# Two token tiles of the expert picks scattered instead of three, and four through the one-hot gates instead of three

## What is computed

```
s1, s2 = q1 @ key1.T, q2 @ key2.T            # 128 scores each
v1, i1 = top_k(s1, 16);  v2, i2 = top_k(s2, 16)
sc, pos = top_k(all 256 sums v1 + v2, 16)
experts = i1[pos // 16] * 128 + i2[pos % 16]
gate = softmax(sc)
act = gelu(u[experts] . x_t) * gate
out_t = sum over picks of act * v[experts]
```

## Time and profile before

| | us |
|---|---|
| median of three runs | 4469.14 (4467.87 to 4476.68) |
| the profiled execution, its own time | 4451.02 |
| its span, first to last instruction | 4449.4 |
| head stage, first query tile to the end of the bridge | 1964.2 to 2484 |
| gate stage, to the last gate matmul | 2484 to 3017 |
| tail | 3017 to 3361 |
| expert sums and final norm | 3361 to 4449 |

### The profile page before, as it was taken

The page is one execution under the profiler, slowest core; times in us unless marked ns, Lnnn a source line. Parts: engine busy times, 40 slices in busy tenths (PEclk is TensorE's granted clock), DMA queues, the critical chain, the costliest instruction groups (busy, mean ns, idle before and its releaser), DMA issues.

```text
span 4449.4 us, 63937 instructions
## 1 busy us (share of the span) xinstructions
PE 4185.1 (94%) x22555; PEld 3563.2 (80%) x22555; DVE 3044.1 (68%) x6114; ACT 1557.6 (35%) x2721; POOL 1466.3 (33%) x1221
## 2 busy tenths in 40 slices
PE   7999999999899889989999998898798999999998
PEld 4668877777688768779999988888797888888886
DVE  7531037777467744447888688885468998888888
ACT  4222226555477633232223444442121222222222
POOL 0000000000044411002888788888753222222220
PEclk9999999999999989999999999999899999999999
DMA  6646323333456465233445699999898988888885
GB/s 266 243 167 244 141 76 130 117 131 113 156 173 191 141 227 184 95 106 93 93 89 108 171 267 261 262 277 273 235 347 315 303 304 285 288 288 285 287 286 197
DMA packets 479233, 913.43 MB, mean 205 GB/s; under 512 B 188818, under 2 KB 270114, under 8 KB 475412
## 3 DMA queue, kind: packets, MB, share of 16 engines
q1 hardware_dynamic: 321524, 509.44, 35.2%
q0 software_dynamic: 151136, 363.35, 27.1%
q10 hardware_dynamic: 6336, 37.75, 2.3%
HBM read 747.38 MB, written 188.17 MB: 210 GB/s over the span
## 4 chain that ended last, share of the span: by engine, by line
PE 34%; POOL 10%; DMA 5%; DVE 4%; issue 2%; ACT 0%; SPq 0%; DVEq 0%; ACTq 0%; POOLq 0%
PE ph_gate_ps L2489 15%; PE ph_hid_ps L2414 9%; PE ph_hid_ps L2489 7%; POOL scratch_scattered L2364 5%; POOL ph_ring L2370 4%; DMA ph_ring<-in_u_rows,held_tiles 4%; PE ph_hid_ps L2404 2%; DVE ph_ring L2795 1%; PE ph_score_ps L2422 1%; DVE held_tiles L2813 1%; DVE ph_u_lo L2621 0%; DMA scratch_scattered<-held_tiles 0%; DVE held_tiles L2809 0%; DVE ph_row_hot L2807 0%; DMA held_tiles<-scratch_scattered 0%
## 5 line engine op out<-in xcount | busy, mean ns | idle before, releaser
L2364 POOL DMA_INDIRECT scratch_scattered<-held_tiles x384 | 670.1, 1745 | 285.9 <-DVEq L2718 151.0
L2414 PE MATMUL ph_hid_ps<-ph_n_hi,ph_u_hi 128*128 128x384 f32 x2048 | 706.1, 345 | 50.3 <-DVE ph_u_lo L2621 50.3
L2414 PE MATMUL ph_hid_ps<-ph_n_lo,ph_u_hi 128*128 128x384 f32 x2048 | 697.3, 340 | 0.0
L2414 PE MATMUL ph_hid_ps<-ph_n_hi,ph_u_lo 128*128 128x384 f32 x2048 | 696.8, 340 | 0.0
L2390 POOL DMA_INDIRECT ph_ring<-in_v_experts,ph_pick_again x256 | 240.0, 937 | 775.5 <-DVE held_tiles L2901 743.4
L2795 DVE CUSTOM_DVE_ANT_0 ph_ring<-ph_ring,ph_n_rows 128x1024 f32<-128x1024 f32 x256 | 309.5, 1224 | 208.9 <-DMA ph_ring<-in_u_rows,held_tiles 207.9
L2414 PEld LDWEIGHTS ph_hid_ps<-ph_n_hi,ph_u_hi 128*128 128x128 f32 x2048 | 395.2, 193 | 55.9 <-DVE ph_u_lo L2621 55.7
L2414 PEld LDWEIGHTS ph_hid_ps<-ph_n_lo,ph_u_hi 128*128 128x128 f32 x2048 | 394.7, 193 | 0.2
L2414 PEld LDWEIGHTS ph_hid_ps<-ph_n_hi,ph_u_lo 128*128 128x128 f32 x2048 | 394.0, 192 | 0.0
L2370 POOL DMA_INDIRECT ph_ring<-in_u_rows,held_tiles x256 | 331.3, 1294 | 142.8 <-DVE held_tiles L2795 85.5
L2901 DVE SCALAR_TENSOR_TENSOR held_tiles<-ph_ring,ph_factor,held_tiles 128x1024 f32<-128x1024 f32 x254 | 325.0, 1280 | 0.0
(11 more groups left out here) (398 smaller groups left out, 9759.7 us busy)
## 6 DMA issues: line engine op xcount, KB each, us to landing
ph_u_raw<-in_tiles SPq DMA_DIRECT2D x136, 512.0 KB
ph_v_raw<-in_v_experts SPq DMA_DIRECT2D x124, 512.0 KB, 4.8
scratch_hidden<-ph_hidden SPq DMA_DIRECT2D x128, 384.0 KB, 3.5
ph_u_raw<-scratch_hidden SPq DMA_DIRECT2D x124, 384.0 KB, 5.0
proj_w_ch<-in_w_ch SPq DMA_DIRECT2D x49, 512.0 KB, 3.7
mb_w_raw<-in_w_branch POOLq DMA_DIRECT2D x48, 512.0 KB, 3.9
scratch_gate_tiles<-ph_gates SPq DMA_DIRECT2D x48, 512.0 KB, 7.9
ph_hidden<-scratch_gate_tiles SPq DMA_DIRECT2D x124, 192.0 KB, 4.0
```

What stands on the lines that cost most here:

```text
L2364: pool.indirect_dma_start(d["scattered"], bass.IndirectOffsetOnAxis(place_of[:, at:at + 1], 0), held[:, 2, GM + at:GM + at + 1], None, com ...
L2414: mm = pe.matmul(hid_halves[r][:, c, :], u[r][a][:, k, :], n2[b][:, k, c * CUT:(c + 1) * CUT], start=(k == 0 and a + b == 0), stop=(k == K ...
```

## The change

ST goes from 3 to 2. With it DT becomes 4, GM 512, the tokens scattered 256; a head has 32 scatters, 256 in all; the gate stage has 32 steps, the tail 16 tiles; the gate stores become 64 of 512 KB, the zeroed buffer 16 MB, not 24 MB (`CLEARS`). Each expert's gate load is 256 KB from `scratch_gate_tiles` and 128 KB from `scratch_scattered`, before 192 and 192. `FIRST_AT` moves to tiles 8, 10, 12, 14 of the shorter tail, and the loads for it to tiles 5 and 11. The pairs of scatter and gather begin at head 6, not 4, so that 192 gathers follow the last scatter, before 64. The eight stores of the last block of gates go out two by two behind the first four tiles of the tail. Dots: from step 12 on a step has 3 + 4, before 3 + 3; the tail has 4 per tile, and 2 at the `FIRST_AT` tiles, so that 206 of the 256 lie in the gate stage (138 before), and the last in tail tile 13, two before its end; before, they lay up to the last tile.

```diff
-                CLEARS = (6, 6, 0)
+                CLEARS = (4, 4, 0)
...
-ST = 3
+ST = 2
...
-        FIRST_AT = (22, 24, 26, 28)
+        FIRST_AT = (8, 10, 12, 14)
...
-                store_gates(BLOCKS - 1, range(PIECES))
...
+                    if y < PIECES // 2:
+                        store_gates(BLOCKS - 1, range(2 * y, 2 * y + 2))
...
-                    if h == PH // 2:
+                    if h == PH - 2:
                         pool.wait_ge(hid_mm[1], PERIOD // 2 * (PH - 2) + 1)
                     for n in range(SCATTERS):
                         scatter(h, n)
-                        if h >= PH // 2:
+                        if h >= PH - 2:
                             gather(next(gathers))
...
-                            dots(3 if j >= 1 else 0)
+                            dots((4 if b == 3 and j >= 12 else 3) if j >= 1 else 0)
...
-                    dots(3 if y in FIRST_AT else 3 + (y % 4 != 0) if y < TAIL - 1 else PICKS)
+                    dots((2 if y in FIRST_AT else 4) if y < TAIL - 1 else PICKS)
```

## The result

| | before | after |
|---|---|---|
| median | 4468.51 us (4466.02 to 4476.68) | 4398.74 us (4397.70 to 4401.41) |
| the profiled execution, its own time | 4451.02 | 4399.33 |
| its span | 4449.4 | 4397.7 |
| last scatter | 3203.9 | 2734.6 |
| last gate matmul | 3016.9 | 3169.9 |

Both medians are of four executions. The ratio is 0.9842, with an interval of 0.9825 to 0.9859: 70 us less, or 1.6%. The forecast was 4437 us, 32 us less. The direction came out and the time lies within the range, but the gain is more than twice the forecast. Between the two profiled executions the gate stage and the tail together are 46.6 us shorter (818.8 us from the first gate matmul to the end of the last expert tile, before 865.4) and the entry into the expert sums 6.5.

A forecast was written before the change was run, and what follows sets the result against it. POOL was taken to set the pace of gate stage and tail until the last scatter; 2755.2 + 419.1 + 161 + 38.8 + 1043.4 = 4417.5 us, plus the profile-to-median difference, gave 4437 us, range 4394 to 4482.

The forecast's parts named there:

- POOL sets the pace: Gate stage and tail until the last scatter: POOL's alternating scatters and gathers, one gather per 3.75 us, make steps about 22.5 us.
- Fewer zero stores, nothing: Stretch of the zero stores: fewer of them gain nothing, since PE was busy 269.43 of 270 us there.
- the 18 us: Whole kernel: profiled execution 18 us below the runs' median of 4469.14, a difference carried over to the forecast time.
- tiles 0 to 3 of the tail, 52 us: First four tail tiles: 16.3 MB at 294 to 328 GB/s takes 50 to 55 us, taken as 52.
- Tiles 4 to 7, 40 us: Next four tail tiles: 16 dots at 2.5 us each, 40 us.
- Two per tile hold SP some 6 us: First four tail tiles: two spread gate stores occupy SP some 6 us under 8.3 of a tile, removing one stall.
- Tiles 8 to 13, 52 us: Later tail: 18 dots (45 us) under 50 us of PE, with four experts' loads; 52 us taken.
- Gate steps, 21.4 us: Gate steps 12 to 31, seven dots: 21.4 us each, floor 20.5 from DVE, other end 22.5; end of step 31 12.5.
- Entry: 38.8 forecast: From tail into expert sums: 38.8 us, not 45.8, by taking 7 of 9.2 us of gaps; bounds 2 and 9.2.
- B: Rival: DMA takes the denser stream, only PE and DVE count; steps 20.5, tail 141, entry 35, 4396 us; chance 0.20.
- C: Rival, slower: DMA engines replace POOL in gate steps 12 to 31, 23.5 us per step, 4491 us; chance 0.15.
- D: Rival: gate steps gain but the tail gives it back, four dots per tile at 11 us, 4461 us; chance 0.13.

The follow-up runs named there:

- half_scatters: The kernel before without the scatters of heads 4 to 7 (192 of 384 left out, so part of the gates is missing): 4355.92 us, ratio 0.9748.
- gathers_from_head4: The changed kernel with the pairs of scatter and gather from head 4 on again, 128 pairs, not 64: 4443.96 us, ratio 0.9948.
- six_dots: The changed kernel with six dots in every gate step and five, not four, per tail tile (two at the four preparations): 4402.99 us, ratio 0.9859.

## Why the prediction was right in sign and half in size

The two profiled executions differ by 51.7 us. The forecast for them was 32. The stages, in us:

| | forecast | measured | difference |
|---|---|---|---|
| start of step 12 | 2755.2 | 2757.0 | +1.8 |
| to the last gate matmul | 419.1 | 412.9 | -6.2 |
| tail | 161 | 144.4 | -16.6 |
| entry | 38.8 | 39.3 | +0.5 |
| expert sums | 1043.4 | 1044.1 | +0.7 |
| span | 4417.5 | 4397.7 | -19.8 |
| added for the median | +19.5 | +1.0 | -18.5 |

- **POOL sets the pace: held.** Pairs ended at 2734.6 (forecast 2738). Steps 1 to 11 stayed at 22.0 us. Taking scatters away (half_scatters) brought PE's pace back, and putting pairs back (gathers_from_head4) took it away again.
- **Fewer zero stores, nothing: held.** The first query tile starts between 1964.2 and 1971.4 in the three traces with twelve such stores, and between 1964.8 and 1973.5 in the eleven with eight.
- **The step that failed first: the 18 us.** The forecast took the distance between one execution and a median of three as a constant of the machine. The kernel before spreads over 31 us, and its profiled execution was at the fast end; the changed one spreads over 6, and its profiled execution was in the middle. Nearly half of the miss is this term. The spread was 31 us over 52 executions with 192 pairs, 9 over six with 128, 7 over four with none (half_scatters), 6 over eight with 64, and 4 to 13 over four or five in each of the other kernels with 64. This fits a POOL pace that varies from execution to execution, and does not show it. In the two traces of before, 7 of 13 us had come up before the first query tile, and that point varies over 9 us in the traces of all kernels. What varies there stays open.
- **The mis-sized term: tiles 0 to 3 of the tail, 52 us by a DMA ceiling of 294 to 328 GB/s.** They took 33.3 us. The 328 GB/s of the earlier trace rows at a share of 0.92 was what that stretch moved, not what it could have had. Tiles 2 to 5 ran at 368 to 372 GB/s, and PE was the bound. This gave 19 us, more than the whole miss of the tail. There was not much above it, though: with a fifth dot per tile (six_dots) PE no longer kept its pace, at 368 GB/s over 74 us.
- **Tiles 4 to 7, 40 us, were right for a wrong reason.** They took 40.3, but 16.6 of it for tiles 4 and 5, at PE's pace, and 23.7 for 6 and 7. Dots at 2.5 us were not the limit: that was a mean over 16 tiles, and in four of them, 19 to 22 (3239.3 to 3272.6), PE had kept its 8.3 us per tile in the kernel before. The late load on SP behind the pairs was. "Two per tile hold SP some 6 us" was 23 divided by four. Under the tail's load three of the four pairs held it 9 to 10 us, and tiles 6 to 9 took 44 us where PE needed 33. Without it the tail would have been PE's 133.
- **Tiles 8 to 13, 52 us:** 53.8, with the rest of the stall in them; behind tile 9 PE was busy 50.16 of 50.3 us.
- **Gate steps, 21.4 us:** 21.0 each, and 14.3 for the end of step 31, not 12.5. The floor of 20.5 held as a floor; DVE's share of 0.97 says it was the bound, and six_dots shows it (390 us).
- **Entry: 38.8 forecast, 39.3 measured**, in part because errors cancel. The factor came 2 us after the tail, as forecast, the first v row 5.5 us later, not 8.4. PE waited 4.17 us, where the forecast left 2.2 of the 9.2, and was busy for 35.08 us, before 36.63.
- **The rivals.** B's price for the tail, 141, was nearly true, its steps of 20.5 and its entry of 35 were not. C was refuted twice. What was said against it was true but small: in 2755:3017 of the kernel before, packets of 8 bytes or less, the scatters' among them, took 0.08 of the share of 0.97. D's place was right (the tail has a stall), its size was not: no stretch of it took 11 us per tile but tiles 6 to 9. Of the Trainium skill's two sentences from DMA: Bandwidth & Descriptors, the one on transfers under 512 B (Specifications) would have given C. The runs disagree in what matters: 256-byte stores did not keep this mix from 311 GB/s, nor the tail's first 50 us, in which all eight stores are issued or begun, from 353. The fit of 2.0 us plus bytes over 436 GB/s (Anatomy of one DMA) gives an estimate of 3.2 us for a gather; the earlier trace rows had 7.2 under load, and the last gather of the chain of waits behind the stall took 11.19 us.

What the stall consists of is not settled. That stores in one run make it longer is shown (155 us for the tail, not 144). The rest, 8 to 13 us over PE's floor in the kernels with spread stores (six_dots aside), could be SP held by the stores, their writes, the experts' loads, or the load on the DMA engines, which moved more there than in any other stretch of the table of windows (387 GB/s). No run divided these.

## What to carry to other kernels

When one engine issues two kinds of transfers in turn, its pace for one kind is the sum of both. Count it against what the consumer needs, and place the second kind beside stretches that another engine bounds; beside a stretch where the consumer has no slack it costs again. A DMA rate read in one stretch is no ceiling for another, and a share near 1 is none either. And a difference between one profiled execution and a median is a sample from a spread: look at the spread before it is carried over.

## What the runs showed of the hardware

- The DMA engines moved 353 GB/s over 50 us and 387 over 44 us of the tail on one core, with 256-byte stores among the transfers. The share reads 1.05 there, and 0.94 to 0.98 at 261 to 311 GB/s in other stretches.
- SP's time to issue a 512 KB store in runs of 256 bytes was not fixed: 2.2 us each in the first pair of the tail, 4.4 to 5.0 in the next three, 3.9 in the run of eight, 2.9 in that of the kernel before. A hidden store issued right behind a pair took 2.2 to 4.6 us in the tail, where it took 0.48 before them (3170.16). That this follows the load on the DMA engines was not tested.
- The granted clock stayed at 1.00 in every long stretch in which PE ran without gaps; it was 0.97 to 0.98 in the POOL-paced gate steps of both kernels, and 0.83 to 0.92 in the windows of the stalls. In gathers_from_head4 it was 0.90 over 231 us, and PE was busy for 194.73 us with nine steps' work, 21.6 us each instead of 19.5: a gap costs its own length and, behind it, some of PE's speed.
